# Turning the feed-forward activations by 32x32 block transposes and four spreading transfers instead of TensorE transposes

## The reference, cut to what matters

```python
def swiglu(h, w_gate_up, w_down):
    g, u = jnp.split(h @ w_gate_up, 2, axis=-1)
    return (jax.nn.silu(g) * u) @ w_down

ff = swiglu(rmsnorm(h, ffn_pre_norm[l]), ffn_w_gate_up[l], ffn_w_down[l])
h = h + rmsnorm(ff, ffn_post_norm[l])
```

## Time and profile before

| | |
|---|---|
| median of 3 runs | 1060.62 us (1060.05 to 1060.73) |
| span of the profiled execution | 1059.6 us |
| TensorE busy | 1049.6 us (99% of the span) |
| VectorE busy | 658.3 us (62%) |
| ScalarE busy | 567.9 us (54%) |
| data moved | 187.78 MB, mean 177 GB/s |
| granted TensorE clock | 0.999 |

### The profile page before, as it was taken

How to read it: one execution, slowest core, us unless ns; L and a number is a source line. 1 busy time by engine, 2 the same in 40 slices (tenths; PEclk the granted TensorE clock), 3 DMA queues, 4 the chain that set the end, 5 groups by cost and what they waited for, 6 DMA issues and landing times.

```text
span 1059.6 us, 14790 instructions
## 1 busy us (share of the span) xinstructions
PE 1049.6 (99%) x5023; PEld 861.5 (81%) x5023; DVE 658.3 (62%) x953; ACT 567.9 (54%) x920; POOL 78.7 (7%) x170
## 2 busy tenths in 40 slices
PE   9999999999999999999999999999999999999997
PEld 6999888888887788888888888888887688888886
DVE  5867855546687874554567455556777675555543
ACT  5755644445577664444556444454666844444543
POOL 0035100000012040000001000000101200000000
PEclk9999999999999999999999999999999999999999
DMA  8574656555653454646565465646543253656541
GB/s 341 179 238 137 204 171 216 164 198 188 204 182 107 135 181 160 222 159 209 184 200 186 165 210 164 218 160 219 184 154 100 97 181 120 215 162 218 166 152 40
DMA packets 51882, 187.78 MB, mean 177 GB/s; under 512 B 5808, under 2 KB 5952, under 8 KB 51840
## 3 DMA queue, kind: packets, MB, share of 16 engines
q1 hardware_dynamic: 50688, 183.79, 52.1%
q0 software_dynamic: 864, 3.07, 1.0%
q10 hardware_dynamic: 288, 0.37, 0.1%
HBM read 186.15 MB, written 1.05 MB: 177 GB/s over the span
## 4 chain that ended last, share of the span: by engine, by line
PE 95%; DVE 3%; ACT 1%; POOL 0%; DMA 0%; issue 0%; DVEq 0%; SPq 0%
PE pG L1684 17%; PE pG L1686 17%; PE pG L1685 17%; PE pD L1684 12%; PE pD L1686 11%; PE pD L1685 11%; PE pT L1689 3%; PE pG L1689 1%; PE pG L1706 1%; DVE w_low L1341 1%; PE pG L1942 1%; PE pT L1827 1%; PE pD L1689 1%; PE pD L1695 0%; PE pD L1961 0%; PE pG L1988 0%
## 5 line engine op out<-in xcount | busy, mean ns | idle before, releaser
L1341 DVE TENSOR_TENSOR w_low<-raw,w_high 128x1024 fp32r<-128x1024 f32 x340 | 410.9, 1224 | 118.5 <-ACT w_high L1055 105.7
L1055 ACT ACTIVATE w_high<-raw 128x1024 fp32r<-128x1024 f32 x340 | 353.8, 1055 | 81.5 <-PE pG L1686 66.5
L1684 PE MATMUL pG<-w_high,xTh 128*128 128x512 f32 (+1 forms) x816 | 320.1, 392 | 0.1
L1686 PE MATMUL pG<-w_high,xTl 128*128 128x512 f32 (+1 forms) x816 | 312.5, 383 | 0.0
L1685 PE MATMUL pG<-w_low,xTh 128*128 128x512 f32 (+1 forms) x816 | 312.1, 382 | 0.0
L1686 PEld LDWEIGHTS pG<-w_high,xTl 128*128 128x128 f32 x816 | 153.1, 188 | 28.3
L1685 PEld LDWEIGHTS pG<-w_low,xTh 128*128 128x128 f32 x816 | 153.6, 188 | 25.7
L1684 PEld LDWEIGHTS pG<-w_high,xTh 128*128 128x128 f32 x816 | 153.2, 188 | 25.6 <-DVE xTl L1374 0.3
L1684 PE MATMUL pD<-w_high,aTh 128*128 128x512 f32 x384 | 150.8, 393 | 0.0
L1686 PE MATMUL pD<-w_high,aTl 128*128 128x512 f32 x384 | 149.9, 390 | 0.0
L1685 PE MATMUL pD<-w_low,aTh 128*128 128x512 f32 x384 | 149.4, 389 | 0.0
(11 more groups left out here) (272 smaller groups left out, 799.4 us busy)
## 6 DMA issues: line engine op xcount, KB each, us to landing
raw<-in_stream SPq DMA_DIRECT2D x340, 512.0 KB, 4.4
post<-in_posts POOLq DMA_DIRECT2D x5, 512.0 KB, 5.1
early<-in_stream SPq DMA_DIRECT2D x4, 512.0 KB, 12.3
first_w<-in_stream SPq DMA_DIRECT2D x3, 512.0 KB, 5.8
h<-in_x SPq DMA_DIRECT2D x2, 512.0 KB, 5.4
out<-hg SPq DMA_DIRECT2D x3, 256.0 KB, 2.2
consts<-in_consts POOLq DMA_DIRECT2D x1, 417.0 KB, 3.8
out<-hg ACTq DMA_DIRECT2D x1, 256.0 KB, 2.9
```

The lines of the kernel that those rows point to most:

```text
L1055: sc.activation(w_high[:, slot(static):slot(static) + CHUNK], raw_of(static), ACT.Copy).then_inc(w_high_done, 1)
L1341: ve.tensor_tensor(w_low[:, slot(static):slot(static) + CHUNK], raw_of(static), w_high[:, slot(static):slot(static) + CHUNK].bitcast(F32), ...
L1684: pe.matmul(dst, ah, hi, start=start, stop=False)
L1686: return pe.matmul(dst, al, hi, start=False, stop=stop)
```

## The change

In the feed-forward phases TensorE does no T. VectorE turns `act` by its 32x32 block transpose into `aB` as the last part of G. A new step M(t, b) on ScalarE waits for `aB` and issues four transfers, each of 32 partitions of `aB` (128 KB in all, in pieces of 256 bytes) spread over the 128 partitions of `aF`. ScalarE's T then waits for the four transfers and copies `aF` to `aTh`, and VectorE's T takes `aTl` from `aF`. The rows of the down weights are laid out in another order on the host to fit. Only T(1, 10) of the fourth phase is still done by TensorE. The order of the steps in a phase becomes:

- TensorE: G(0, b+1), D(0, b), G(1, b), D(1, b-1).
- ScalarE and VectorE, from the start of G(1, b): R of its first chunk, T(1, b-1), R of two chunks, M(0, b+1), G(1, b), R of the fourth chunk, T(0, b+1), R of two down chunks, M(1, b), G(0, b+2).

SyncE now walks the same order of steps, with the same condition for each load. The mixer's order is as before.

```diff
+def walk_ffn_step(ph, s, shift, step, freed, open_end=None):
+
+    step("G", 0, s, shift)
+    if s == 0:
+        step("M", 0, 0, shift)
+        if open_end:
+            open_end()
+            refill(step, freed, 1)
+            step("join", 1, ph.index - 1)
+            step("T", 0, 0, shift)
+            refill(step, freed, 2)
...
+    step("D", 0, s - 1, shift)
+    refill(step, freed)
+    walk_ffn_follower(ph, s - 1, shift, step)
+
+
+def walk_ffn_follower(ph, b, shift, step):
+
+    g, first, last = ph.g_chunk(b), b == 0, b == ph.nb - 1
+    early = 2 if first else 3
+    step("R", g, 1, shift)
+    if not first:
+        step("T", 1, b - 1, shift)
+    step("R", g + 1, early - 1, shift)
+    if not last:
+        step("M", 0, b + 1, shift)
+    step("G", 1, b, shift)
+    step("R", g + early, ph.cg - early, shift)
+    if not last:
+        step("T", 0, b + 1, shift)
+    if not first:
+        step("D", 1, b - 1, shift)
+    if not first and not last:
+        step("R", ph.d_chunk(b - 1), ph.kd, shift)
+    step("M", 1, b, shift)
...
@@ walk_last_follower
-    step("T", 1, b, 0)
     if ph.mixer:
+        step("T", 1, b, 0)
         step("Y", 1, b, 0)
-    refill(step, freed, 2 if ph.mixer else 3)
+        refill(step, freed, 2)
+    else:
+        step("M", 1, b, 0)
+        refill(step, freed, 2)
+        step("T", 1, b, 0)
+        refill(step, freed, 1)
...
@@ the end of a phase
     step("D", 0, last, 0)
     step("tail", 0, ph.index)
+    step("T", 1, last - 1, 0)
     step("join", 0, ph.index)
...
@@ ScalarE
                 else:
-                    sc.activation(aTh[t][:].rearrange("p k r -> p (k r)"), pT[t][:, 0:256], ACT.Copy).then_inc(ah_ready[t], 1)
+                    if t == 1 and b:
+                        sc.wait_ge(w_freed, freed_by(ph, b - 1, True) + shift * RING)
+                    if moved_by_pe(ph, t, b):
+                        sc.wait_ge(actT_psum[t], MIX.nb + 1)
+                    else:
+                        sc.wait_ge(aF_moved[t], ffn_block(ph, b, shift) * 64)
+                    sc.activation(aTh[t][:].rearrange("p k (a r) -> p k a r", a=4), turned_act(ph, t, b), ACT.Copy).then_inc(ah_ready[t], 1)
...
+            def M(t, b, shift, ph):
+
+                if moved_by_pe(ph, t, b):
+                    return
+                sc.wait_ge(aB_ready[t], ffn_block(ph, b, shift))
+                for a in range(4):
+                    sc.dma_start(aF[t][:, 64 * a:64 * a + 64], aB[t][32 * a:32 * a + 32, :]).then_inc(aF_moved[t], 16)
...
@@ VectorE
+                    if not moved_by_pe(ph, t, b):
+                        ve.wait_ge(act_ready[t], n)
+                        ve.transpose(aB[t][:], act[t][:]).then_inc(aB_ready[t], 1)
...
@@ TensorE
+                if b and not ph.mixer:
+                    pe.wait_ge(act_ready[t], ph.first_block + b + shift * (RING // (ph.cg + ph.kd)))
...
+                if not ph.mixer and not moved_by_pe(ph, t, b):
+                    return
```

More of the change, by code:

```diff
@@ L153, in refill, with walk_block_step @@
         step("R", freed.pop(0), 1, 0)
-def walk_block_step(ph, s, shift, step, freed, open_end=None):
+def walk_block_step(ph, s, shift, step, freed):
     def fill(name):
-        if ph.mixer and (name, s) in FILL:
+        if (name, s) in FILL:
             step("fill", FILL[name, s], 1)
-    if not (ph.mixer and s == 0):
+    if s:
         step("G", 0, s, shift)
-    if ph.mixer and s == 1:
+    if s == 1:
         step("G", 1, 0, shift)
[L166 to L174, removed]
     if s == 2:
@@ L178, in walk_block_step @@
         fill("Y10")
[L179 to L182, removed]
+        step("Y", 1, 0, shift)
     if s >= 1:
@@ L258, in last_product, with walk_mixer @@
     freed += range(ph.d_chunk(ph.nb - 1), ph.d_chunk(ph.nb - 1) + ph.kd)
-def walk_phase(eng, ph, step, trips, freed, open_end=None):
-    per = RING // (ph.cg + ph.kd)
[L264 to L272, removed]
+def walk_mixer(ph, step, freed):
+    for s in range(ph.nb):
+        walk_block_step(ph, s, 0, step, freed)
+    step("D", 0, ph.nb - 1, 0)
+    step("tail", 0, ph.index)
+    step("join", 0, ph.index)
+    walk_last_follower(ph, step, freed)
@@ L273, in walk_phase, with walk_ffn @@
+def walk_ffn(eng, ph, step, trips, freed, open_end=None):
+    per = RING // (ph.cg + ph.kd)
+    for s in range(3):
+        walk_ffn_step(ph, s, 0, step, freed, open_end)
+    with eng.Fori(0, trips) as turn:
+        for s in range(3, 3 + per):
+            walk_ffn_step(ph, s, turn, step, freed)
+    for s in range(3 + per * trips, ph.nb):
+        walk_ffn_step(ph, s, 0, step, freed)
     last = ph.nb - 1
     if ph is FFN4:
-        walk_follower(ph, last, 0, step, freed)
+        walk_ffn_follower(ph, last, 0, step)
+        step("T", 1, last, 0)
@@ L870, in _ @@
-            for c in range(turns * RAW, N_CHUNKS):
-                sp.wait_ge(w_split, c - RAW + 1)
-                i = c % RAW
-                sp.dma_start(raw[:, i * CHUNK:(i + 1) * CHUNK], stream[FIRST + c]).then_inc(w_loaded[i], 16)
-            for ready, count, t, half in ((out_by_act, 1, 0, 0), (out_by_act, 2, 0, 1), (out_by_dve, 1, 1, 1)):
-                sp.wait_ge(ready, count)
-                sp.dma_start(out_half(t, half), hg[t][:, 512 * half:512 * half + 512]).then_inc(out_stored, 16)
@@ new lines, in fill, with refill, finish @@
+            def fill(first, n, ph):
+                for c in range(first, first + n):
+                    load_behind(c, 0)
+            def refill(first, n, shift, ph):
+                for c in range(first + RING, first + RING + n):
+                    if c < N_CHUNKS:
+                        load_behind(c, shift)
+            def finish(ph):
+                for ready, count, t, half in ((out_by_act, 1, 0, 0), (out_by_act, 2, 0, 1), (out_by_dve, 1, 1, 1)):
+                    sp.wait_ge(ready, count)
+                    sp.dma_start(out_half(t, half), hg[t][:, 512 * half:512 * half + 512]).then_inc(out_stored, 16)
+                sp.wait_ge(out_stored, 64)
@@ L880, in _ @@
+            steps = dict(start=start, fill=fill, R=refill, finish=finish)
+            walk(sp, lambda name, *a, ph=None: steps[name](*a, ph) if name in steps else None)
         @block.gpsimd
```

123 lines of the change are left out of this document (67 added, 56 removed).

## The result

The changed kernel takes 1094.5 us (median of 4 runs, 1092.1 to 1096.5) beside 1060.7 us before: a ratio of 1.0315, 95% interval 1.0296 to 1.0335. It is slower by 34 us where 1058.3 was forecast. The time lies outside the range of 1049 to 1077.

The account below looks back on a forecast made before the run. TensorE, busy 99% of the span, was taken to bound the kernel. Terms -22.6 + 0 + 3.3 + 8.0 + 0.2 + 8.8 = -2.3 us gave 1057.3 from 1059.6, 1058.3 as median; range 1049 to 1077.

Parts of the forecast that it names:

- Removed turns: TensorE, 87 steps T removed at 0.26 us each: -22.6 us (-12 to -24).
- The issue: ScalarE, each M: four issues of 0.36 us, 1.4 us of its queue.
- which ScalarE has: ScalarE's queue: 87 M take 125 us, for which there is room, as ScalarE is 54% busy.
- The landing in the middle: T(0, b+1) in mid-phase: fourth transfer lands 9.9 after G(1, b) starts, 1.1 us before the deadline 11.0; cost 0 us.
- the first rival: Mid-phase, T(0, b+1), 36 times: transfers land late beside the weight loads; 1098, or 1076 halfway; chance 0.24.
- Leaving, D(0, 10): End of three phases: TensorE waits 1.1 us each, from VectorE's queue; +3.3 us (+3 to +8).
- Leaving, D(1, 10): End of first and third phase: waits of 4.0 us each, +8.0 (+7 to +9.5); second phase +0.2.
- Entering: G(1, 0) of three phases: waits for xTl of 3.8, 2.7 and 2.3; together +8.8 us (+6 to +10).
- The third rival: Behind each T: splits, not TensorE, set the pace, so removing turns gains nothing; 1060; chance 0.02.
- the second, that the ends cost less: Ends of phases: only half of the 20 us is paid, 1048, or a third, 1045; chance 0.17.

Follow-up runs that it names:

- e1: The changed kernel without the four transfers of every M, T copying straight from aB, so activations not fully turned: 1050.6 us.
- e8: The kernel whose transfers SyncE issues, with one spare ScalarE copy of 1024 columns in the place of each M: 1061.5 us.
- e11: The kernel whose transfers SyncE issues, with two spare ScalarE copies of 1024 columns in the place of each M: 1074.3 us.
- e6: The changed kernel with the four transfers issued by SyncE, once the block transpose is done, and not by ScalarE: 1055.4 us.
- e14: The changed kernel with SyncE issuing, M(0, b+1) at the late place, and two spare ScalarE copies in place of each M: 1077.7 us.
- e3: The changed kernel with 15 spare TensorE matmuls ahead of D(0, 10) (three phases) and D(1, 10) (first and third phase): 1084.6 us.
- e13: The kernel before the change, ScalarE held up by four spare copies ahead of T(1, 10)'s high part in first and third phase: 1073.2 us.
- e15: The changed kernel, ScalarE still issuing, but T copies from aB and landings are hardly awaited; activations not fully turned: 1071.2 us.
- e7: The changed kernel with SyncE issuing the transfers and the last block of each phase turned by TensorE: 1044.6 us.

## Why the prediction was wrong

**The sign.** It forecast -2.3 us; it is +34. Three steps failed: the price of an issue, the landing at D(0, 10), and the clock, which was left out. By its own steps:

**Removed turns: right.** -22.6 forecast, about -21.4 by e1. A middle step fell by 0.46 us, as the earlier trace rows let expect.

**The issue: mis-sized.** 0.36 us was taken from one store to memory; it measured 0.625, so an M lasts 2.5 us and not 1.4. The text had both ends for whether issues run beside an activation (they do, as taken), but none for the price of an issue itself; it only named one over 0.45 as a sign of being wrong. Its "which ScalarE has" looked at a mean over the kernel: ScalarE is 52% busy, and yet one copy per M in its queue cost 6 us (e8) and two cost 18.9 (e11). At the ends of phases TensorE's next product stands behind them: D(0, 10) starts 2.4 us late in e11 and 0.8 in e6, D(1, 10) 4.8 and 5.1 against 2.7 and 2.9. In the middle of the changed kernel the gate moves by 1.2 us, from 5.77 after zero to 6.99.

**The landing in the middle: mechanism seen, value too low.** 9.9 after zero was forecast, 10.84 came: 0.7 us from the longer issues, and a last transfer of 4.6 us. That is just inside the deadline of 11.0, which the trace bears out: most middle steps don't wait, and TensorE stands still in 11 places, for 1.4 us at most. Together that is 6.7 us, where 0 was taken; the other 1.4 us by which the table's last row grew are starts at half clock. This is the first rival, with its cause: the transfers meet the loads of the earlier trace rows. Its span of 1076 to 1098 holds the time, but its place was wrong, as it put all 36 waits in the middle. The ends of the range were too narrow for it as well: the bad ends of the forecast's own terms already add up to +15.7 us, or 1076, where the text has 1065, and the 1077 said to reach to the middle of this rival stands at the lower end of its 1076 to 1098. By the Trainium skill ("DMA: Bandwidth & Descriptors", Queues, rings and completion order) each DMA engine takes turns between queues, a packet at a time, by which small pieces would wait for weight pieces. The landing beside the loads (3.0 to 4.6 us) and that ahead of two of them in one queue (1.9 to 3.0) agree with it, though no run here shows the packets' order. The same page (Issuing engines are not separate DMA queues) has it that issuing on several engines saves no more than the time to issue. Here the runs differ: with the queue time roughly made up for and M(0, b+1) in the same place, SyncE's transfers, ahead of two loads, left the kernel 17 us shorter than ScalarE's (e14 against the changed kernel).

**Leaving, D(0, 10): a step contradicted itself.** 1.1 us was taken, from VectorE's queue. But the text's own landing of 9.9, a high and a low part of 0.4 each, makes 10.7 against a start at 8.2: 2.5 us each. The walk left out the landing at the very place where nothing covers it. With the true landing 3.9 to 4.4 came.

**Leaving, D(1, 10): right by two errors that cancel.** 8.2 was forecast, 8.5 came. The issues there lasted 1.1 us longer than in the walk, but they began before the last square on ScalarE had run and not behind it, 1.2 us before its end (first phase):

```profile
297.36 0.55 ACTq L1248 DMA_DIRECT2D aF<-aB  x1
...
298.41 0.19 ACT L1148 ACTIVATION_READ_ACCUMULATOR junk<-h 128x1 f32 x1
...
298.60 1.28 ACTq L1248 DMA_DIRECT2D aF<-aB  x2
```

So M ended 1.3 us behind the square's end, where the walk had 1.2. The high and low parts behind it took 3.9 us, where the walk had 4.0.

**Entering: right in size, not in place.** 3.8, 2.7 and 2.3 us were forecast, all for `xTl` at G(1, 0); 2.4, 2.7 and 2.7 came. In the first phase TensorE waited for `w_low`, in the other two for `h` first (1.6 and 0.5) and then for `xTl` (1.1 and 2.2).

**The clock: left out.** The sum treated a wait of TensorE as its own length. Some 15 us at half clock came on top (the 18.9 above, less what fell on TensorE standing still), and e3 gave 10 of the 34 us back. No stretch of the kernel before, but for its end, showed the lower level, so no row had warned of it; a wait of 4 us was itself a forecast, and what follows one was never asked. e3 and e13 show that cause from both sides: work in the wait keeps the clock up, and a wait without any transfer brings it down. The Trainium skill ("TensorE: Matmul & The Clock Gate", Why this matters for your kernels) warns of just this, that idle gaps between bursts of matmuls bring the lower level back; the rows of e13 agree, and the prediction did not draw on it.

**The places in the 39 us** (e6 against the changed kernel): queue time 18.9, place 1.8 (3.3 on top of the queue time), and the 17 that are left, which the rows of e14 and e15 put down to transfers that land late beside the loads, with half clock behind. The split is rough, since copies stood in for issues. The third rival, that turns cost nothing, is out by e1, and the second, that the ends cost less, by the table above.

## What to carry to other kernels

Before work leaves the engine that bounds a kernel for a DMA, look at the issuing engine's queue: price an issue by one of the same kind, ask what stands behind it, and issue it from a queue that has time to spare, as soon as its data is there and ahead of the large loads. Where TensorE otherwise never stands still, a few waits of 4 us cost about one and a half times their length (12.5 us for 8.3 in e13). At ends of phases, where a result is wanted at once, the short path (here TensorE's own transpose) is worth its time; in the middle the long one costs next to nothing (e7, 1.5% faster than before).

## What the hardware showed that I had not expected

- An issue of a transfer between SBUF tiles took 0.625 us in the median on ScalarE and 0.603 on SyncE, with 256-byte pieces or whole rows (0.612), where ScalarE's store to memory had taken 0.358. The first of four started beside a running activation.
- Spare work on TensorE during a wait makes a kernel faster (e3, by 10 us).
- Stops of about 4 us and more came with half clock in the profiles of these runs, all 20 of them. With shorter ones it varied: start to start 2.90 and 3.12 us at D(1, 10) in e6 and in e1, in the same places; the clock fell in e6 and stayed in e1. Rows of e6, then of e1:

```profile
290.00:295.00 5.00, 2.96 (x10) 2.33 (x11) 3.49 (x5) 2.15 (x5) 0.00 (x0) 0.85 0.59 192
295.00:300.00 5.00, 5.00 (x20) 4.05 (x19) 3.10 (x6) 1.92 (x4) 0.85 (x2) 0.81 0.31 123
```

```profile
290.00:295.00 5.00, 4.18 (x18) 3.49 (x19) 3.00 (x5) 1.61 (x5) 0.29 (x1) 1.00 0.81 266
295.00:300.00 5.00, 5.00 (x28) 4.21 (x27) 4.34 (x8) 2.58 (x5) 0.81 (x2) 1.00 0.12 48
```

What tells the two apart was not settled.
